# Row projections of a two-mixer block: two of 512 columns in place of four of 256

## The chip, the cores and the metric

The kernel runs on one core of one Trainium2 chip. The metric is the device time of one launch in microseconds (us). The kernel before the change has a median of 2136.6 us over 3 runs (2136.44 to 2136.79).

## The reference

The program computes a block of two layers and then a second block of another kind, for 512 tokens of width 1024, in fp32. The change touches only the mixers of the two layers of the first block:

```
h = rms_norm(x, attn_norm_w[layer])
proj = h @ w_in[layer]              # 1024 -> 12 groups of 256 columns
a_q, a_i, a_zf, a_zb, a_g, b_u, c_q, c_k, c_v = split(proj)   # 256 each, the three c_* 512
o_a = hgrn2_mixer(a_q, a_i, a_zf, a_zb, a_g, lb)   # gated recurrence, both directions, chunks of 64
o_b = fourier_mixer(b_u)                           # real part of a 2-D DFT
o_c = dilated_attention_mixer(c_q, c_k, c_v)       # rotary on q and k, softmax attention
x = x + concat(o_a, o_b, o_c) @ w_out[layer]
x = x + square(relu(rms_norm(x) @ w_up[layer])) @ w_down[layer]
```

Most results of the projection are wanted with channels on the partitions. Three are wanted with tokens on the partitions ("rows"): `a_i` (the values of the recurrence), `b_u` (input of the DFT) and `c_v` (the values of the attention), 1024 columns in all.

## The kernel before, in words

**Projections.** fp32 products are made of three fp32r products. ScalarE copies each weight tile to a rounded part (`WH`, function `act_hi`), VectorE subtracts it from the raw weight for the rest (`WL`, `dve_lo`), and TensorE adds high*high, low*high and high*low. A weight *chunk* is 128 x 2048 (1 MB); SyncE loads it into one of two `raw` slots. A chunk is two *units* of 1024 columns, and there are three places for finished units (`NUNIT = 3`): unit u can be made once TensorE has let go of unit u-3. ScalarE and VectorE make a unit 1.06 and 1.2 us at a time, and TensorE waits for it by the semaphore `w_lo`. A projection (`lin`) of 256 columns takes one chunk.

`pe_lin` works in four *projection steps* of 12 matmuls of 512 columns: unit 0 into result tile 0, unit 0 into tile 1, then unit 1 into each. `pe_rows`, where the tokens are the stationary operand and the weights move, also has four steps, of 24 matmuls of 256 columns. In both a unit is let go after two steps, so a new unit is wanted every second step.

**One mixer.** Its projections are, in order: `head` = two gates, two silu, and the rows of `a_i`; `tail` = two for q, two for k (kind `copy`), the rows of `b_u`, and two rows projections for `c_v`. That is 12 projections, 24 units (numbered 0 to 23 here) and 48 projection steps (0 to 47). Units 8 and 9 are those of `a_i`, 10 to 17 those of q and k, 18 and 19 those of `b_u`, 20 to 23 those of `c_v`. ScalarE evicts rows from PSUM with a factor per token (`act_made`).

Beside them runs the recurrence, as sixteen *level steps*: levels -1 to 6, in two halves each (`rec_pe`, `rec_act`, `rec_dve`, `rec_pool`). In a level step TensorE makes scores (16 matmuls of 128 columns), VectorE merges them (`copy_predicated`, line 154) and makes the operands of the next level from exponentials of ScalarE. At level 6 ScalarE, not VectorE, evicts the scores. Then follow four transposes-and-sum steps: the turned keys ("kt", which ScalarE evicts), the chunk states ("st", which needs `a_i`), the outputs ("o"), the sums and the inverse roots. After the last projection step come the DFT (`four_pe`) and the attention.

**What sets the order.** Each engine has an order of its own, written out by hand as a string: a `u` is one step of the projections and what goes with them, a `c` one step of the recurrence. TensorE follows `MIX_PE`, VectorE `MIX_DVE`, ScalarE and GpSimd `MIX`. On ScalarE and VectorE every second `u` has work: evict the finished projection (if there is one) and make one unit, two ahead. So in the last two groups of the eight, ScalarE's order is: level 5 first half (the two exponentials for level 6), level 5 second half, evict q/k, unit 18; level 6 first half (evict its scores), unit 19; level 6 second half, evict, unit 20. VectorE's is: level 4 second half, low part of unit 17; level 5 first half, low part of 18; level 5 second half; level 6 first half, low part of 19. TensorE's is: steps 32, 33; level 5 first half; 34; level 5 second half; 35, 36; level 6 first half; 37; level 6 second half; 38, 39, 40; kt; 41; st; 42, 43, 44; o; 45; sum; 46, 47; DFT.

**The rotary exchange.** q and k are multiplied in place, and their halves of 32 partitions are exchanged by DMAs of SyncE (`sp_turn`, line 1458), which stand in SyncE's queue between the chunk loads: after the load of chunk n comes the exchange of projection n-3. The rotation works of VectorE and GpSimd stand at fixed units (`ROT = 14`).

**Banks.** A projection has two of the four PSUM banks 0 to 3, by the parity of its number (`BANK`). `clear` waits until the bank's last holder is evicted, and `four_pe` waits for the last rows projections in the same way before it writes banks 0 to 3.

Of the kernel before, what the change touches and what calls it, by code (L numbers as in the profile page):

```python
# [12 lines left out]
ACT = mybir.ActivationFunctionType  # L13
# [210 lines left out]
def build(nc, I, out):  # L224
    ctx = ExitStack()
    with ctx:
# [82 lines left out]
        def lin(src, kind, to=None, j=0, ly=0):  # L309
            lins.append(Lin(len(lins), [chunk(x) for x in src], kind, to, j, ly))  # L310
            return lins[-1]
# [13 lines left out]
        def mix_memory(ly):  # L325
# [37 lines left out]
            m.ms, m.rs, m.ris = (small[:, 256 + 32 * i:288 + 32 * i] for i in range(3))  # L363
            W = I["w_in"][ly]
            m.head = [lin([W[2, 0]], "gate", j=0, ly=ly), lin([W[3, 0]], "gate", j=1, ly=ly),
                      lin([W[0, 0]], "silu", m.aq2, ly=ly), lin([W[4, 0]], "silu", m.ag2, ly=ly),
                      lin([W[1, 0]], "rows", m.ai3, ly=ly)]
            m.tail = [lin([W[6 + j, 0]], "copy", m.cq3[:, 2 * j:2 * j + 2], ly=ly) for j in range(2)]
            m.tail += [lin([W[8 + j, 0]], "copy", m.ck3[:, 2 * j:2 * j + 2], ly=ly) for j in range(2)]
            m.tail += [lin([W[5, 0]], "rows", m.u3, ly=ly)]  # L370
            m.tail += [lin([W[10 + j, 0]], "rows", m.cv3[:, :, 256 * j:256 * j + 256], ly=ly) for j in range(2)]
            m.dft = chunk(I["dft"], "raw")
            m.out = [lin([I["w_out"][ly][j, 0]], "res", (m.scratch, 2 * ly), j, ly) for j in range(4)]
            f = m.ffn = Mix()
# [127 lines left out]

        BANK, BEFORE, holder = {}, {}, {}
        for l in lins:
            for m in range(2):
                b = (2 * (l.n - s2.low[0].n) + m) % 3 if l.kind in ("lat", "shift", "keep") else l.n % 2 * 2 + m
                BANK[l.n, m], BEFORE[l.n, m] = b, holder.get(b)
                holder[b] = (l, m)

# [34 lines left out]
        def pe_lin(e, l):  # L544
            for ci, n in enumerate(l.chunks):
                u0 = chunks[n][2]
                for h in range(2):
# [4 lines left out]
                    for m in range(2):  # L552
# [15 lines left out]
                            t.then_inc(*did("w_use", u))  # L568
                        yield

        def pe_rows(e, l):

            u0 = chunks[l.chunks[0]][2]
            for h in range(2):
                e.wait_ge(*at("w_lo", u0 + h))
                wh, wl = unit(u0 + h)
                for m in range(2):
                    if h == 0:
                        clear(e, l, m)
                    for tk in (2 * m, 2 * m + 1):  # L580
                        o = bank_of(l, m)[:, tk % 2 * 256:(tk % 2 + 1) * 256]
                        for k in range(4):
                            xh, xl, made = operand(l, h * 4 + k)
                            e.wait_ge(*at(*made))
                            xh, xl = xh[:, tk * 128:(tk + 1) * 128], xl[:, tk * 128:(tk + 1) * 128]
                            ws = slice(k * 256, (k + 1) * 256)
                            e.mm(o, xh, wh[:, ws], h + k + tk % 2 == 0, False)
                            e.mm(o, xl, wh[:, ws], False, False)
                            t = e.mm(o, xh, wl[:, ws], False, h + k + tk % 2 == 5)
                    if h:  # L590
                        t.then_inc(*did("lin_mm", l.n, m))
                    elif m:
                        t.then_inc(*did("w_use", u0))
                    yield

        def pe_lins(e, ls):
            for l in ls:
                yield from pe_rows(e, l) if l.kind == "rows" else pe_lin(e, l)

        def act_made(e, l):  # L600

            for m in range(2):
                ps = bank_of(l, m)
                if l.kind in ("gate", "silu"):
                    sg = mixes[l.ly].sg[m]
                    e.wait_ge(*at("lin_dve", "ps", l.n, m))
                    if l.kind == "silu":
                        p = lins[l.n - 1]
                        e.wait_ge(*at("lin_dve", "sg" if p.kind == "gate" else "out", p.n, m))
                    e.act(sg, sg if l.kind == "gate" else l.to[:, m, :], ACT.Sigmoid).then_inc(*did("lin_act", "sg", l.n, m))  # L610
                elif l.kind == "rows":
                    e.wait_ge(*at("lin_mm", l.n, m))
                    e.wait_ge(*at("nrm_dve", 2 * l.ly - 1, "col"))
                    for i in range(2):
                        t = e.act(l.to[:, 2 * m + i, :], ps[:, i * 256:(i + 1) * 256], ACT.Copy,
                                  rcol[:, 2 * m + i:2 * m + i + 1])
                    t.then_inc(*did("lin_act", "ps", l.n, m))
                elif l.kind == "copy":
                    e.wait_ge(*at("lin_mm", l.n, m))
                    e.act(l.to[:, m, :], ps, ACT.Copy).then_inc(*did("lin_act", "ps", l.n, m))  # L620
                elif l.kind == "keep":
                    e.wait_ge(*at("lin_dve", "ps", l.n, m))
                    e.act(s2.keep[m], s2.keep[m], ACT.Sigmoid).then_inc(*did("lin_act", "keep", l.n, m))
                elif l.kind == "hid":
                    f, half = l.to
                    t = 2 * l.j + m
                    e.wait_ge(*at("ffn_dve", l.ly, half, "sq", t))
                    e.act(f.hh[:, t, :], f.rl[m], ACT.Copy).then_inc(*did("ffn_act", l.ly, half, "hi", t))
                elif l.kind == "res" and l.to[1] is not None:
                    act_next(e, l, m)  # L630
# [121 lines left out]
        def side_lins(e, ls, made, split, late):  # L752
# [3 lines left out]
            for l in ls:  # L756
                for n in l.chunks:
                    for h in range(2):
                        if late:
                            yield  # L760
                        if before is not None:
                            made(e, before)
                            before = None
                        u = chunks[n][2] + h + 2
                        if u < len(units) and units[u][0] <= n + 1:
                            split(e, u)
# [145 lines left out]
        def rec_pe(e, x):  # L912
# [32 lines left out]
                        t = e.tr(b[:, ch * 128:(ch + 1) * 128], x.kl[dr][:, (hp * 4 + ch) * 128:(hp * 4 + ch + 1) * 128], ident)  # L945
                    t.then_inc(*did("rec_pe", ly, "kt", dr, hp))
            yield
            e.wait_ge(*at("lin_act", "ps", x.head[4].n, 1))
            for dr in range(2):
                for hp in range(2):  # L950
                    e.wait_ge(*at("rec_act", ly, "kt", dr, hp))
# [268 lines left out]
        def four_pe(e, x, first_scores):  # L1220
# [4 lines left out]
            for part in range(2):  # L1225
                w = slot(n)[:, part * 768:(part + 1) * 768]
                for d in range(2):
                    b, ds = bk(part * 2 + d), slice(d * 128, (d + 1) * 128)
                    l = x.tail[-1 if part else -2]
                    e.wait_ge(*emptied(l, 1))  # L1230
                    e.wait_ge(*emptied(x.tail[-1], 1))
                    e.mm(b[:, 0:128], x.u04[:, ds], w[:, 0:128])
                    e.mm(b[:, 256:384], x.u24[:, ds], w[:, 128:256])
                    for k in range(2):
# [273 lines left out]
        def win_pool(e, x):  # L1508
            yield from between(range(48), **{f"s{ROT + i}": lambda i=i: rot_pool(e, x, i) for i in range(8)})

        MIX = "u" * 12 + "c" + "uu" + "cucuu" * 8 + "cuu" * 4 + "cuuuc"
        MIX_DVE = "u" * 12 + "c" + "uu" + "cuucu" * 8 + "cuu" * 4 + "cuuuc"
        MIX_PE = "u" * 16 + "c" + "cucuu" * 8 + "cu" * 2 + "cuuu" + "cu" + "cuuuc"

# [1517 lines left out]
        def sp_program(e):  # L3032
# [5 lines left out]
            for n in range(2, len(chunks)):  # L3038
# [15 lines left out]
                if 0 <= fixed < 4:  # L3054
                    for i in range(2 * fixed, 2 * fixed + 2 + fixed // 3):
                        sp_expert(e, i)
                if n - 3 in lin_of_chunk and lin_of_chunk[n - 3] in turned_lins:
                    sp_turn(e, lin_of_chunk[n - 3])
                if n < s2.wr2_c[0] and n - 3 in lin_of_chunk and lin_of_chunk[n - 3].kind == "keep":
                    sp_keep(e, lin_of_chunk[n - 3])  # L3060
            for k in range(4):
# [255 lines left out]
def layout(inp):  # L3317
# [6 lines left out]
    a["w_out"] = np.stack([lay(g["w_out"][i], 8, 256) for i in range(2)])  # L3324
    a["w_up"] = np.stack([lay(g["w_up"][i], 8, 256) for i in range(2)])
    a["w_down"] = np.stack([lay(g["w_down"][i], 8, 256) for i in range(2)])
    q = {k[:-2]: x[0] for k, x in g.items() if k.endswith("_2")}
    a["pos2"] = np.ascontiguousarray(g["positions_2"][0])
    w = q["w_in"]
# [42 lines left out]
```

## Time and profile before

| what | us |
|---|---|
| median of three runs | 2136.6 |
| the profiled execution's own time | 2136.76 |
| its span, first to last instruction | 2135.0 |
| TensorE busy | 2072.6 (97%) |
| VectorE busy | 1183.8 (55%) |
| ScalarE busy | 734.7 (34%) |
| GpSimd busy | 133.1 (6%) |
| mean granted TensorE clock | 0.991 of full speed |
| layer 0: steps of the recurrence beside the projections | 59.79 to 185.11 |

Times inside the profile are counted from the start of the span. In a row of the timeline the first number is the start, the second the length, xN the number of instructions merged in it, and [x <-engine tile line] says that the engine sat idle for x us before it and what ended that. A row's count depends on where the asked stretch ends, its start doesn't. Matmuls overlap (each is shown some 0.39 us long and the next starts 0.23 us later), so a distance is read from start to start.

### The profile page before, as it was taken

To read this page: it belongs to the slowest core of one execution; us is meant where nothing else is said; L and a number is where in the kernel's file an instruction comes from. 1 tells how busy PE (TensorE), PEld (TensorE's weight loads), DVE (VectorE), ACT (ScalarE), POOL (GpSimd) and SP (SyncE) were. 2 spreads that over 40 slices of the span, in tenths; PEclk is the share of its full clock that TensorE was granted. 3 is DMA by queue.
4 is the path that set the end of the run, shared out by engine and by line. 5 is a ranking of instruction groups with operands and counts; after the bars stand their busy time and mean duration, and the time that the engine had idled before them with its cause. 6 is when DMAs were issued, how large, how long until landed. Compare 5 with 4: busy or idle time off the path is not lost.

```text
span 2135.0 us, 32294 instructions
## 1 busy us (share of the span) xinstructions
PE 2072.6 (97%) x13784; PEld 1561.1 (73%) x13784; DVE 1183.8 (55%) x1878; ACT 734.7 (34%) x1139; POOL 133.1 (6%) x112
## 2 busy tenths in 40 slices
PE   8999999999999999999999999999999999999997
PEld 6886688888888886688888887566688856944543
DVE  8886555435535886555325445475743345444545
ACT  6445642212233445633212333234422123311112
POOL 1220010000010220010000020000000000100000
PEclk9999999999999999999999999999999999999998
DMA  5222022222222222022222222211211036299993
GB/s 194 70 83 76 11 95 99 99 99 99 99 91 86 70 85 80 21 81 97 99 99 99 99 99 79 85 56 56 78 61 62 32 129 261 106 419 419 379 420 155
DMA packets 47139, 263.08 MB, mean 123 GB/s; under 512 B 7064, under 2 KB 7320, under 8 KB 18960
## 3 DMA queue, kind: packets, MB, share of 16 engines
q1 hardware_dynamic: 44400, 256.46, 32.3%
q0 software_dynamic: 2160, 4.17, 0.5%
q8 instruction: 111, 1.82, 0.4%
q10 hardware_dynamic: 432, 0.34, 0.1%
q14 instruction: 36, 0.29, 0.0%
HBM read 251.01 MB, written 9.44 MB: 122 GB/s over the span
## 4 chain that ended last, share of the span: by engine, by line
PE 86%; DVE 8%; ACT 3%; issue 1%; DMA 1%; SPq 0%; DVEq 0%; ACTq 0%; POOLq 0%
PE psum L121 83%; DVE A_mix L134 3%; PE psum L124 2%; ACT A_mix L128 1%; DVE WL L134 1%; DVE A_second L134 1%; ACT A_mix L131 1%; DVE A_second L142 1%; DVE A_mix L160 1%; ACT WH L128 1%; DVE A_mix L154 1%; DMA A_mix<-A_mix 0%; DMA experts<-h_rows,A_second 0%; SPq L166 0%; DVE HL L134 0%
## 5 line engine op out<-in xcount | busy, mean ns | idle before, releaser
L134 DVE TENSOR_TENSOR WL<-raw,WH 128x1024 fp32r<-128x1024 f32 x236 | 300.9, 1277 | 351.5 <-ACT WH L128 351.0
L128 ACT ACTIVATE WH<-raw 128x1024 fp32r<-128x1024 f32 x236 | 247.5, 1054 | 355.5 <-PE psum L121 340.0
L121 PE MATMUL psum<-HH,WH 128*128 128x512 f32 x736 | 299.7, 407 | 17.7 <-DVE HL L142 10.2
L121 PE MATMUL psum<-R_op,WH 128*128 128x512 f32 x1024 | 315.9, 390 | 0.0
L121 PE MATMUL psum<-R_ffn,WH 128*128 128x512 f32 x1024 | 315.1, 389 | 0.0
L121 PE MATMUL psum<-HL,WH 128*128 128x512 f32 x736 | 288.5, 392 | 0.0
L121 PE MATMUL psum<-HH,WL 128*128 128x512 f32 x736 | 288.4, 392 | 0.0
L121 PEld LDWEIGHTS psum<-R_op,WH 128*128 128x128 f32 x1024 | 192.2, 188 | 40.7 <-issue 1.0
L121 PEld LDWEIGHTS psum<-R_ffn,WH 128*128 128x128 f32 x1024 | 192.2, 188 | 40.0
L121 PE MATMUL psum<-R_ffn,WL 128*128 128x512 f32 x512 | 199.2, 389 | 0.0
L121 PE MATMUL psum<-R_op,WL 128*128 128x512 f32 x512 | 199.2, 389 | 0.0
L121 PEld LDWEIGHTS psum<-HH,WH 128*128 128x128 f32 x736 | 138.9, 189 | 63.9 <-DVE WL L134 16.6
L121 PEld LDWEIGHTS psum<-HH,WL 128*128 128x128 f32 x736 | 139.0, 189 | 30.0
L121 PEld LDWEIGHTS psum<-HL,WH 128*128 128x128 f32 x736 | 139.3, 189 | 28.6 <-issue 1.9
L121 PE MATMUL psum<-A_second 64*64 64x64 f32 (+4 forms) x3736 | 154.1, 233 | 5.5 <-DVE A_second L154 2.5
L121 PEld LDWEIGHTS psum<-A_second 64*64 64x64 f32 (+3 forms) x3736 | 124.3, 137 | 35.4 <-issue 23.7
L121 PE MATMUL psum<-A_mix 128*64 128x128 f32 (+4 forms) x1408 | 126.0, 315 | 7.8 <-DVE small L160 3.7
L128 ACT ACTIVATE A_second<-psum 128x512 f32<-128x512 f32 (+3 forms) x109 | 52.4, 502 | 194.0 <-PE psum L121 177.8
L134 DVE TENSOR_TENSOR A_mix<-A_mix 128x512 f32<-128x512 f32 (+2 forms) x150 | 112.5, 800 | 10.2 <-DMA A_mix<-A_mix 8.7
L121 PEld LDWEIGHTS psum<-R_op,WL 128*128 128x128 f32 x512 | 96.1, 188 | 20.0
L121 PEld LDWEIGHTS psum<-R_ffn,WL 128*128 128x128 f32 x512 | 96.1, 188 | 19.9
L121 PEld LDWEIGHTS psum<-A_mix 128*64 128x64 f32 (+2 forms) x1408 | 80.3, 161 | 37.3 <-issue 19.2
(217 smaller groups left out, 2662.3 us busy)
## 6 DMA issues: line engine op xcount, KB each, us to landing
raw<-in_w_in SPq DMA_DIRECT2D x41, 1024.0 KB, 4.9
raw<-in_w_up SPq DMA_DIRECT2D x32, 1024.0 KB, 4.9
raw<-in_w_down SPq DMA_DIRECT2D x32, 1024.0 KB, 4.9
A_second<-in_w_gu SPq DMA_DIRECT2D x31, 1024.0 KB, 15.0
A_second<-in_w_dn SPq DMA_DIRECT2D x23, 1024.0 KB, 18.8
experts<-in_w_gu SPq DMA_DIRECT2D x23, 1024.0 KB, 15.5
raw<-in_w_out SPq DMA_DIRECT2D x12, 1024.0 KB, 4.9
X<-in_w_gu SPq DMA_DIRECT2D x10, 1024.0 KB, 17.0
```

The lines of the kernel that those rows point to most:

```text
L121: return self.raw.matmul(o, l, r, start=start, stop=stop)
L124: return self.raw.matmul(o, i, ident, is_transpose=True, start=True, stop=True)
L128: return self.raw.activation(o, i, f, scale=scale)
L131: return self.raw.activation(o, i, f, scale=scale, bias=bias, accum_out=accum)
L134: return self.raw.tensor_tensor(o, a, b, op)
L142: return self.raw.scalar_tensor_tensor(o, a, s, b, op0, op1)
L154: return self.raw.copy_predicated(o, m, a)
L160: return self.raw.tensor_tensor_reduce(o, a, b, scale, 3.0e38, ADD, MIN, accum)
```

## The change

The four rows projections of a layer become two of 512 columns each, behind q and k: the first gives `a_i` and `b_u` together, the second all of `c_v`. Their weights come from a new array `w_row` (the same bytes in another layout, in chunks of 4 times 128 rows by 512 columns, two chunks per projection). Projections per layer are 10, chunks, units and projection steps stay 12, 24 and 48: q and k now take units 8 to 15, the rows units 16 to 23 (steps 32 to 47).

`pe_rows` now has eight steps for its four units, each step one unit into two token tiles, 12 matmuls of 512 columns, in the order `ROW_PIECES` (unit, first tile): a rows projection uses all four banks. The pairs of tiles finish in the order (2, 3), (0, 1). ScalarE evicts tiles 2 and 3 at the projection's last unit (`act_rows`) and 0 and 1 with the next projection's first.

`MIX` (ScalarE and GpSimd) has its seventh group changed from `cucuu` to `uuccu`: two `u` are moved ahead of level 5. `MIX_DVE` and `MIX_PE` are as they were. The exchange stands after the load of chunk n for projection n-4. The recurrence's states and the DFT wait for the new projections.

```
-                      lin([W[0, 0]], "silu", m.aq2, ly=ly), lin([W[4, 0]], "silu", m.ag2, ly=ly),
-                      lin([W[1, 0]], "rows", m.ai3, ly=ly)]
+                      lin([W[0, 0]], "silu", m.aq2, ly=ly), lin([W[4, 0]], "silu", m.ag2, ly=ly)]
             m.tail = [lin([W[6 + j, 0]], "copy", m.cq3[:, 2 * j:2 * j + 2], ly=ly) for j in range(2)]
             m.tail += [lin([W[8 + j, 0]], "copy", m.ck3[:, 2 * j:2 * j + 2], ly=ly) for j in range(2)]
-            m.tail += [lin([W[5, 0]], "rows", m.u3, ly=ly)]
-            m.tail += [lin([W[10 + j, 0]], "rows", m.cv3[:, :, 256 * j:256 * j + 256], ly=ly) for j in range(2)]
+            for j, to in enumerate(((m.ai3, m.u3), (m.cv3,))):
+                m.tail.append(lin([I["w_row"][ly, j, k] for k in range(2)], "rows", to, ly=ly))
...
+        ROWS = (2, 3, 0, 1)
+        ROW_PIECES = ((0, 0), (1, 0), (0, 2), (1, 2), (2, 2), (3, 2), (2, 0), (3, 0))
         def pe_rows(e, l):
+            us = [chunks[n][2] + h for n in l.chunks for h in range(2)]
+            for i, tk0 in ROW_PIECES:
+                e.wait_ge(*at("w_lo", us[i]))
+                wh, wl = unit(us[i])
+                for tk in (tk0, tk0 + 1):
+                    if i == 0:
+                        clear(e, l, tk)
+                    o, ts = bank_of(l, tk), slice(tk * 128, (tk + 1) * 128)
+                    for k in range(2):
+                        xh, xl, made = operand(l, 2 * i + k)
+                        ws = slice(k * 512, (k + 1) * 512)
+                        e.mm(o, xh[:, ts], wh[:, ws], i + k == 0, False)
+                        e.mm(o, xl[:, ts], wh[:, ws], False, False)
+                        t = e.mm(o, xh[:, ts], wl[:, ws], False, i == 3 and k == 1)
+                    if i == 3:
+                        t.then_inc(*did("lin_mm", l.n, tk))
+                    elif tk == (3, 3, 1)[i]:
+                        t.then_inc(*did("w_use", us[i]))
+                yield
...
+        def act_rows(e, l, tks):
+            e.wait_ge(*at("nrm_dve", 2 * l.ly - 1, "col"))
+            for tk in tks:
+                ps, w = bank_of(l, tk), S // len(l.to)
+                e.wait_ge(*at("lin_mm", l.n, tk))
+                for i, to in enumerate(l.to):
+                    t = e.act(to[:, tk, :], ps[:, i * w:(i + 1) * w], ACT.Copy, rcol[:, tk:tk + 1])
+                t.then_inc(*did("lin_act", "ps", l.n, tk))
...
+                        if made is act_made and l.kind == "rows" and (n, h) == (l.chunks[-1], 1):
+                            act_rows(e, l, ROWS[:2])
...
-            e.wait_ge(*at("lin_act", "ps", x.head[4].n, 1))
+            e.wait_ge(*at("lin_act", "ps", x.tail[4].n, 1))
...
-                    l = x.tail[-1 if part else -2]
-                    e.wait_ge(*emptied(l, 1))
-                    e.wait_ge(*emptied(x.tail[-1], 1))
+                    e.wait_ge(*emptied(x.tail[-1], 1 if part else 3))
...
-        MIX = "u" * 12 + "c" + "uu" + "cucuu" * 8 + "cuu" * 4 + "cuuuc"
+        MIX = "u" * 12 + "c" + "uu" + "cucuu" * 6 + "uu" + "ccu" + "cucuu" + "cuu" * 4 + "cuuuc"
...
-                if n - 3 in lin_of_chunk and lin_of_chunk[n - 3] in turned_lins:
-                    sp_turn(e, lin_of_chunk[n - 3])
+                if n - 4 in lin_of_chunk and lin_of_chunk[n - 4] in turned_lins:
+                    sp_turn(e, lin_of_chunk[n - 4])
```

## Rows read from the trace of the kernel before

**Rows 1.** The page: span, TensorE's busy time, and the chain that ended last

```profile
span 2135.0 us, 32294 instructions
...
PE 2072.6 (97%) x13784; PEld 1561.1 (73%) x13784; DVE 1183.8 (55%) x1878; ACT 734.7 (34%) x1139; POOL 133.1 (6%) x112
...
PE 86%; DVE 8%; ACT 3%; issue 1%; DMA 1%; SPq 0%; DVEq 0%; ACTq 0%; POOLq 0%
```

**Rows 2.** Groups by form: the matmuls of 256 columns, one of three alike

```profile
L121 PE MATMUL psum<-WH,HH 128*128 128x256 f32 x256 | 74.2, 290 | 0.0
```

**Rows 3.** Timeline of TensorE, layer 0, levels and projections

```profile
63.94 0.83 PE L121 MATMUL psum<-A_mix 64*128 64x128 f32 x10
...
70.98 1.16 PE L121 MATMUL psum<-A_mix 64*128 64x128 f32 x16
...
77.64 0.50 PE L121 MATMUL psum<-HH,WH 128*128 128x512 f32 x1 [1.35 <-DVE WL L134]
...
98.15 1.16 PE L121 MATMUL psum<-A_mix 64*128 64x128 f32 x16
...
104.91 1.16 PE L121 MATMUL psum<-A_mix 64*128 64x128 f32 x16
...
126.51 0.71 PE L121 MATMUL psum<-A_mix 64*128 64x128 f32 x8
...
130.55 1.16 PE L121 MATMUL psum<-A_mix 64*128 64x128 f32 x16
...
137.88 1.16 PE L121 MATMUL psum<-A_mix 64*128 64x128 f32 x16 [0.35 <-DVE A_mix L134]
...
142.04 1.16 PE L121 MATMUL psum<-A_mix 64*128 64x128 f32 x16
...
151.87 1.94 PE L124 MATMUL psum<-C,A_mix 128*128 128x128 f32 x16
...
156.60 1.62 PE L121 MATMUL psum<-A_mix 128*64 128x64 f32 x48
...
167.27 0.80 PE L121 MATMUL psum<-A_mix 128*64 128x128 f32 x8 [0.22 <-DVE A_mix L142]
...
185.11 2.86 PE L121 MATMUL psum<-raw,A_mix 128*128 128x128 f32 x16 [1.02 <-ACT A_mix L128]
```

**Rows 4.** The same view in layer 1: the DFT's first matmuls

```profile
823.85 1.33 PE L121 MATMUL psum<-raw,A_mix 128*128 128x128 f32 x7 [1.02 <-ACT A_mix L128]
```

**Rows 5.** Timeline of VectorE, layer 0: low parts of units 17 and 19

```profile
124.34 1.21 DVE L134 TENSOR_TENSOR WL<-raw,WH 128x1024 fp32r<-128x1024 f32 x1
...
141.72 1.22 DVE L134 TENSOR_TENSOR WL<-raw,WH 128x1024 fp32r<-128x1024 f32 x1 [2.66 <-ACT WH L128]
```

**Rows 6.** Timeline of ScalarE, layer 0: evictions and high parts

```profile
139.04 1.56 ACT L128 ACTIVATE A_mix<-psum 64x256 f32<-64x256 f32 x4 [6.87 <-PE psum L121]
140.63 1.06 ACT L128 ACTIVATE WH<-raw 128x1024 fp32r<-128x1024 f32 x1
...
154.43 1.60 ACT L128 ACTIVATE A_mix<-psum,small 128x256 f32<-128x256 f32 x4
158.93 2.01 ACT L128 ACTIVATE WH<-raw 128x1024 fp32r<-128x1024 f32 x2 [2.90 <-DMA raw<-in_w_in]
```

**Rows 7.** Timeline of TensorE, two long waits elsewhere in the program

```profile
1518.36 0.50 PE L121 MATMUL psum<-HH,WH 128*128 128x512 f32 x1 [2.86 <-DVE A_second L134]
...
2094.19 6.59 PE L121 MATMUL psum<-experts 128*64 128x512 f32 x16 [3.27 <-issue]
```

**Rows 8.** Windows: busy PE, PEld, DVE, ACT, POOL (count), then clock, DMA, GB/s

```profile
1380.00:1385.00 5.00, 3.08 (x10) 1.52 (x9) 3.71 (x5) 0.00 (x0) 0.00 (x0) 1.00 0.37 125
1385.00:1390.00 5.00, 5.00 (x18) 3.11 (x17) 4.93 (x8) 1.06 (x1) 0.00 (x0) 1.00 0.81 298
...
1520.00:1525.00 5.00, 5.00 (x17) 3.91 (x16) 3.92 (x5) 4.16 (x6) 0.00 (x0) 0.67 0.24 93
...
2095.00:2100.00 5.00, 5.00 (x14) 1.58 (x12) 0.00 (x0) 0.00 (x0) 0.00 (x0) 0.50 0.11 44
```

More of the change, by code:

```diff
@@ L504, in build @@
         for l in lins:
-            for m in range(2):
-                b = (2 * (l.n - s2.low[0].n) + m) % 3 if l.kind in ("lat", "shift", "keep") else l.n % 2 * 2 + m
+            for m in range(4 if l.kind == "rows" else 2):
+                b = (2 * (l.n - s2.low[0].n) + m) % 3 if l.kind in ("lat", "shift", "keep") else (l.n % 2 * 2 + m) % 4
                 BANK[l.n, m], BEFORE[l.n, m] = b, holder.get(b)
@@ L569, in pe_lin @@
                         yield
+        ROWS = (2, 3, 0, 1)
+        ROW_PIECES = ((0, 0), (1, 0), (0, 2), (1, 2), (2, 2), (3, 2), (2, 0), (3, 0))
         def pe_rows(e, l):
[L573 to L594, printed above, removed]
@@ new lines, in pe_rows @@
+            us = [chunks[n][2] + h for n in l.chunks for h in range(2)]
[8 more added lines that the diff above has]
+                        xh, xl, made = operand(l, 2 * i + k)
+                        e.wait_ge(*at(*made))
+                        ws = slice(k * 512, (k + 1) * 512)
[7 more added lines that the diff above has]
+                yield
@@ L598, in pe_lins @@
                 yield from pe_rows(e, l) if l.kind == "rows" else pe_lin(e, l)
+        def act_rows(e, l, tks):
[6 more added lines that the diff above has]
+                t.then_inc(*did("lin_act", "ps", l.n, tk))
         def act_made(e, l):
+            if l.kind == "rows":
+                act_rows(e, l, ROWS[2:])
+                return
             for m in range(2):
@@ L610, in act_made @@
                     e.act(sg, sg if l.kind == "gate" else l.to[:, m, :], ACT.Sigmoid).then_inc(*did("lin_act", "sg", l.n, m))
[L611 to L617, printed above, removed]
                 elif l.kind == "copy":
@@ L3326, in layout @@
     a["w_down"] = np.stack([lay(g["w_down"][i], 8, 256) for i in range(2)])
+    a["w_row"] = np.stack([lay(np.concatenate([w[:, 256:512], w[:, 1280:1536], w[:, 2560:3072]], 1), 4, 512)
+                           for w in (g["w_in"][i] for i in range(2))])
     q = {k[:-2]: x[0] for k, x in g.items() if k.endswith("_2")}
```

## The prediction

> **What bounds the kernel now.** Start with the page [rows 1]: TensorE is busy for 97% of the span and the chain that ended last lies on it for 86%, so a change pays by what it takes from TensorE's time, and costs by what it makes TensorE wait. That is an average over stages, so the second view is TensorE's timeline of one mixer [rows 3]. From 63.94 to 185.11 us the engine has four waits, all small: 1.35 us at 77.64 for a unit's low part, 0.35 at 137.88 for an operand of level 6, 0.22 at 167.27 for a chunk state and 1.02 at 185.11 for an eviction ahead of the DFT. Layer 1 repeats it 638.7 us later [rows 4], so one layer is worked out and doubled. The third view is how near VectorE and ScalarE are. The low part of unit 19 ends at 142.94 (141.72 + 1.22) [rows 5], and TensorE's step 38, its first user, begins some 1.1 us behind the level step at 142.04 [rows 3]: 0.2 us to spare. That near miss decides this case. Unit preparation is just in time, so a schedule that wants a unit one step sooner waits.
>
> **The matmuls.** 768 matmuls of 256 columns (three forms of 256, one shown [rows 2]) become 384 of 512, with the same columns streamed. Their cost can't be read from the mean of 290 ns, since neighbours overlap; it is read between starts. From the level step at 63.94 to the one at 70.98 are one level step and two projection steps of 48 matmuls of 256: 7.04 us. From 98.15 to 104.91 are the same with 24 of 512: 6.76 us [rows 3]. So a replaced pair saves 0.28 / 24 = 11.7 ns, 192 pairs of a layer 2.2 us, both layers 4.5 us. One step of 512 is 6.76 - 4.04 = 2.72 us (4.04 is 126.51 to 130.55, a level step and one step), which leaves 1.32 for a level step with its switch.
>
> The Trainium skill ("TensorE: Matmul & The Clock Gate", the section on 56 ns against 53.3 ns) puts the fixed part of a start-to-start distance at about 2.5 ns for a warm matmul. By that, the 384 removed matmuls are worth 1.0 us, an estimate, and the time below would be 3.5 us higher. The trace shows 11.7 ns, and for this pattern the trace is taken.
>
> **Where the new steps want their units.** Before, every unit had two steps, so unit 17 was wanted at step 34, unit 19 at step 38. With `ROW_PIECES` the units of a rows projection are wanted at its steps 0, 1, 4 and 5: unit 16 at step 32, 17 at 33, 18 at 36, 19 at 37, then 20 at 40, 21 at 41, 22 at 44, 23 at 45. Each second unit comes a step early. TensorE's and VectorE's lists are unchanged, so I walk layer 0 through the level steps.
>
> *To 119.75.* `a_i`'s four steps become q's, worth 0.5 us (0.28 for two, 0.11 for each single one). But the wait at 77.64 hangs on evictions and a unit on ScalarE and VectorE, which only partly move with TensorE. I let 0.35 us through (bounds 0 and 0.5), and VectorE's later work, which waits on level steps several times, moves with it.
>
> *Unit 17.* Its low part ended at 125.55 (124.34 + 1.21) [rows 5]; in VectorE's unchanged list it stands behind the merges of level 4's second half. Less 0.35 it is there at 125.2. Step 33 would have begun at 126.51 - 0.35 - 2.72 = 123.4. TensorE waits 1.8 us, and a step after a wait takes 4.04 - 1.1 = 2.95, so level 5 begins at 125.25 + 2.95 = 128.2 instead of 126.51. Bounds: 1.2 (if VectorE's rotation ahead of it shrinks) to 2.2.
>
> *Level 6.* Two level steps and three steps later (4.04 and 6.76) its first half begins at 139.0 instead of 137.88: the wait of 0.35 there is gone and step 36 is shorter. The two `u` that `MIX` moves ahead of level 5 bring unit 18 forward. ScalarE made it behind two exponentials, now before, so it is no longer late for step 36.
>
> *Unit 19.* This is the costly one. On ScalarE the unit's high part stands behind the eviction of level 6's first half, in the old list and in the new one: the changed group ends a `u` before it. Its chain is fixed: TensorE's scores begin at 137.88, the eviction runs from 139.04 to 140.60, the high part from 140.63 to 141.69 [rows 6], the low part from 141.72 to 142.94 [rows 5]. That is 5.06 us from the scores' start. Before, step 37 and the other half of the level filled this time. Now step 37 itself wants unit 19, and in TensorE's strict order level 6's second half, whose inputs are there, stands behind it. Step 37 would begin 1.1 us after the scores' start, so TensorE idles 4.0 us. The second half begins at 139.0 + 5.1 + 2.95 = 147.05 instead of 142.04. Bounds: 3.7 to 4.3.
>
> *Then* the distances go on with the shorter steps: to "kt" 1.32 + 3 x 2.72 = 9.48, so 156.5 (before 151.87); to "st" 4.73 - 0.11 = 4.62, so 161.15 (156.60); to "o" 10.67 - 0.35 - 0.22 = 10.1, so 171.25 (167.27); to the DFT 17.84 less 0.4 for three steps and less the wait of 1.02, so 187.7 (185.11) [rows 3]. That last wait goes because part 0 of the DFT now asks only for tiles 2 and 3, evicted two steps before the end. Net 2.6 us per layer later: about 3.4 won, 6.0 lost.
>
> **What could be late next, costed at nothing.** "st" now needs `a_i`, evicted behind kt: in the old trace four evictions of this kind end at 156.03 (154.43 + 1.60), 4.2 us after kt began [rows 6], and TensorE comes to "st" 4.6 us after it; a slip costs up to 1 us. Units 20 and 21 hang on the second half of level 6 and move with it; by the same durations they are ready about 1.4 us before steps 40 and 41. Unit 22's chunk lands late already (ScalarE waited 2.90 us for it at 158.93 [rows 6]), and with the exchange's rotations pushed some 3 us it is ready near 164.3 against step 44 at 168. SyncE's queue keeps its order: the exchange moves one projection and one chunk, so it stands behind the same load as before, and asks for results that are there sooner. GpSimd's rotation of tile 2 now comes before level 6's product and adds about 1.5 us to it; the product is wanted at 139 and is there near 135.
>
> **The clock.** TensorE has two long waits elsewhere [rows 7]: 2.86 us, after which the window 1520 to 1525 has a granted clock of 0.67, and 3.27 us, after which 2095 to 2100 has 0.50, the lower level of 1.2 GHz throughout [rows 8]. The wait of 1.9 us between 1380 and 1385 (3.08 of 5 us busy) left it at 1.00 [rows 8]. A wait of 4.0 us in a dense stage is longer than both that were followed by a fall, so I charge one fall for unit 19: 5 x (1 - 0.67) = 1.65 us, bounds 0 and 2.5 (5 x 0.50). For unit 17's 1.8 us I charge none. The Trainium skill (the same page, its section on HAM oscillation) warns of just this: TensorE starts again at half rate after an idle gap between bursts. The two rows agree.
>
> Sum per layer 2.6 + 1.6 = 4.2 us, both 8.3 us with rounding. Against the profiled execution's own 2136.76 (span 2135.0) that is 2145.1; that execution is 0.16 above the median, so 2145.0.
>
> **Rivals.**
> *Waits without a fall of the clock:* +5.1, 2141.7. For it: the falls may depend on where a wait lies. Against: both long waits of the trace had one.
> *The first wait lowers the clock too, or the later units slip by as much:* 3.2 more, 2148.1. Against: the wait of 1.9 us that cost nothing.
> *Only unit 19's wait:* unit 17 is in time and TensorE is held 0.5 us by level 6's operand instead; no fall. 2.6 - 2.0 + 0.5 = 1.1 per layer, 2138.7.
> *Faster, no wait at the early units:* the shorter matmuls and the freed eviction come through. It holds if ScalarE makes unit 19 ahead of level 6's eviction, at least 4 us sooner than its list as I read it allows. Then a layer gains 2.6 - 2.0 + 0.5 - 3.9 = -2.8, the time is 2130.9. For it: a third place lets unit 19 be made as soon as unit 16 is let go, after step 34, and its chunk is there. Against: engines here take their work in order, and eviction and high part stand 0.03 us apart in that order [rows 6].
>
> **How the numbers follow.** Forecast 0.48, waits without a fall 0.16, more falls or slips 0.14, only unit 19's wait 0.10, faster 0.12. A measurement of this kernel tells 0.2% (4.3 us) from no change. Slower: 0.48 + 0.14 and 0.13 of the second case, 0.75. Same: the rest of it and most of the fourth, 0.12. Faster 0.13. The range 2138.5 to 2149.5 leaves out the faster case, nearly half of the fourth and a tail above; the likeliest case alone is 2143 to 2147.5.
>
> **What would show it.** In TensorE's timeline after: a wait of about 1.8 us, ended by `WL`, near 125 and one of about 4.0 us near 140 to 144, the same two 640 us later, followed by a window of clock 0.6 to 0.8 near 145 to 150; no wait before the DFT; forms of 256 columns gone and 128 more of each of three forms of 512; ScalarE's high part of unit 19 right behind four evictions. If the span is about 6 us shorter and these waits are missing, the reading of ScalarE's order is wrong. If they are there and the time is under 2141, the clock's share is.

## The result, and the profile after

The changed kernel is slower: median 2142.03 us over 7 runs (2141.28 to 2147.55), the kernel before 2135.28 over 7 (2130.13 to 2136.79). The ratio is 1.0041, with a 95% interval of 1.0031 to 1.0052, so 6.6 to 11.1 us. It is worked out from all executions and not from the two medians, which are 6.8 us apart; the means, 2143.2 and 2134.4, are 8.8 apart. A second group of runs gave 1.0052 (1.0039 to 1.0065). The forecast was 8.3 us more than before and 2145.0; the profiled execution took 2146.67.

The page first: fewer matmuls, TensorE as busy as before, a longer span. Busy TensorE says nothing of what was lost.

```profile
span 2144.9 us, 31518 instructions
...
PE 2074.8 (97%) x13400; PEld 1545.2 (72%) x13400; DVE 1185.1 (55%) x1878; ACT 733.8 (34%) x1131; POOL 134.4 (6%) x112
```

TensorE's timeline of layer 0 answers to [rows 3]. The columns are start, length, what ran, and in brackets the idle time before it with what ended it:

```profile
59.11 1.16 PE L121 MATMUL psum<-A_mix 64*128 64x128 f32 x16
...
63.15 1.05 PE L121 MATMUL psum<-A_mix 64*128 64x128 f32 x14
...
69.91 1.16 PE L121 MATMUL psum<-A_mix 64*128 64x128 f32 x16
...
77.22 0.51 PE L121 MATMUL psum<-HH,WH 128*128 128x512 f32 x1 [2.10 <-DVE WL L134]
...
84.48 1.16 PE L121 MATMUL psum<-A_mix 64*128 64x128 f32 x16
...
126.80 0.50 PE L121 MATMUL psum<-WH,HH 128*128 128x512 f32 x1 [1.76 <-DVE WL L134]
...
129.74 1.16 PE L121 MATMUL psum<-A_mix 64*128 64x128 f32 x16
...
140.54 1.16 PE L121 MATMUL psum<-A_mix 64*128 64x128 f32 x16
...
145.68 0.50 PE L121 MATMUL psum<-WH,HH 128*128 128x512 f32 x1 [3.98 <-DVE WL L134]
...
150.22 1.16 PE L121 MATMUL psum<-A_mix 64*128 64x128 f32 x16
...
190.63 0.60 PE L121 MATMUL psum<-raw,A_mix 128*128 128x128 f32 x4
```

The two waits stand where they were forecast: 1.76 us for unit 17 (1.8 forecast), 3.98 us for unit 19 (4.0). The level steps at 63.15 and 69.91 are 6.76 us apart (7.04 before), and no wait stands before the DFT. Layer 1 has the same two:

```profile
769.39 0.50 PE L121 MATMUL psum<-WH,HH 128*128 128x512 f32 x1 [1.78 <-DVE WL L134]
...
789.83 0.79 PE L121 MATMUL psum<-WH,HH 128*128 128x512 f32 x1 [3.98 <-DVE WL L134]
```

Unit 19's chain, ScalarE's timeline and VectorE's row behind it, answers to [rows 5, 6]. The eviction begins when TensorE has made the scores, the high part 0.02 us behind it, the low part behind that; 145.63 is the end, and 145.68 TensorE's start:

```profile
141.73 1.56 ACT L128 ACTIVATE A_mix<-psum 64x256 f32<-64x256 f32 x4 [10.28 <-PE psum L121]
143.31 1.06 ACT L128 ACTIVATE WH<-raw 128x1024 fp32r<-128x1024 f32 x1
...
144.40 1.23 DVE L134 TENSOR_TENSOR WL<-raw,WH 128x1024 fp32r<-128x1024 f32 x1 [2.94 <-ACT WH L128]
```

ScalarE had idled for 10.28 us before it. That its list alone held it back is what `early19` below shows.

The windows answer to [rows 8] (busy PE, PEld, DVE, ACT, POOL, then the granted clock, DMA share, GB/s). The clock falls behind the waits of 3.98 us in both layers, and in this execution behind the wait of 2.10 us near 77 and that of 1.78 us near 769 too. Behind unit 17's 1.76 us in layer 0 it stays at 1.00:

```profile
75.00:80.00 5.00, 2.90 (x11) 2.26 (x9) 4.83 (x8) 3.14 (x3) 0.00 (x0) 0.80 0.00 2
80.00:85.00 5.00, 5.00 (x25) 3.85 (x26) 3.13 (x5) 2.89 (x4) 1.83 (x2) 0.86 0.62 210
...
125.00:130.00 5.00, 3.24 (x17) 2.44 (x18) 5.00 (x9) 0.82 (x1) 0.00 (x0) 1.00 0.09 22
...
145.00:150.00 5.00, 4.32 (x12) 3.31 (x12) 4.97 (x6) 1.38 (x3) 0.00 (x0) 0.66 0.18 41
...
770.00:775.00 5.00, 5.00 (x28) 3.67 (x26) 2.95 (x5) 2.11 (x2) 0.45 (x1) 0.66 0.22 52
...
790.00:795.00 5.00, 5.00 (x12) 3.63 (x12) 4.47 (x5) 0.53 (x2) 0.00 (x0) 0.52 0.22 52
```

At the DFT layer 0 is 5.5 us late (190.63 against 185.11). The forecast without clock is 2.6 of it, and two falls of 1.6 us are the rest but for 0.3. The falls can be read from the distances: from the end of the wait near 77 to the next level step it is 7.26 us (77.22 to 84.48) against 5.67 before, and from the end of unit 19's wait to level 6's second half 4.54 us (145.68 to 150.22), against 2.94 behind unit 17's wait, where the clock stayed up. Two rows of the kernel before belong to this, its first level step and the one behind the wait:

```profile
59.79 1.16 PE L121 MATMUL psum<-A_mix 64*128 64x128 f32 x16
...
83.31 1.16 PE L121 MATMUL psum<-A_mix 64*128 64x128 f32 x16
```

Counted from the first level step (59.11 and 59.79), the layer takes 6.2 us longer: the 0.7 us by which TensorE came sooner to this stage went into the longer wait near 77.

### The profile page after: what moved, and what is told of

The parts are those of the page before. It is cut to its first block, busy times and chain, and to the rows that moved or that the text cites. A ratio compares the mean times of both kernels' runs of the same rounds, so it can differ in the third digit from the quotient of the medians.

```text
span 2144.9 us, 31518 instructions
## 1 busy us (share of the span) xinstructions
PE 2074.8 (97%) x13400; PEld 1545.2 (72%) x13400; DVE 1185.1 (55%) x1878; ACT 733.8 (34%) x1131; POOL 134.4 (6%) x112
## 3 DMA queue, kind: packets, MB, share of 16 engines
q8 instruction: 108, 1.77, 0.3%
## 4 chain that ended last, share of the span: by engine, by line
PE 86%; DVE 7%; ACT 4%; DMA 1%; issue 1%; SPq 0%; DVEq 0%; ACTq 0%; POOLq 0%
PE psum L121 84%; PE psum L124 2%; DVE A_mix L134 1%; DVE WL L134 1%; ACT A_mix L128 1%; DVE A_second L134 1%; ACT A_mix L131 1%; ACT WH L128 1%; DVE A_second L142 1%; DMA M<-in_m 1%; DVE A_mix L160 0%; DMA experts<-h_rows,A_second 0%; DVE A_mix L154 0%; ACT branch_gates L131 0%; DVE HL L134 0%
```

## The experiments

Each is compared with the kernel before on the same chip; ratios are those of the times, worked out from all executions. "Faster than the changed kernel" goes by the difference of two such ratios. A stretch of a trace is one execution. The theory is that of the prediction: units wanted a step early, and places in the lists. The rivals are named with each run.

**The changed kernel again** (`same`), no edit.

> The changed kernel again, as the anchor of this group. Both theories: 5 to 8 us slower than before, with TensorE waits of 1.8 and 4.0 us in layer 0 for the low parts of units 17 and 19, and the same in layer 1.

2144.56 us, 1.0052. The waits in its trace are 1.77 and 3.98 us. This is the anchor for the three runs that follow (`two_steps`, `fill`, `mix_old`).

**Two steps for each unit** (`two_steps`).

```
-ROW_PIECES = ((0, 0), (1, 0), (0, 2), (1, 2), (2, 2), (3, 2), (2, 0), (3, 0))
+ROW_PIECES = ((0, 0), (0, 2), (1, 0), (1, 2), (2, 2), (2, 0), (3, 2), (3, 0))
```

> ROW_PIECES with two steps in a row for each unit, as in the kernel before; all else of the change stays. Theory (units wanted a step early): the waits for units 17 and 19 are gone, 5.8 us per layer less waiting. But tiles 2 and 3 of the first rows projection then finish one step later (step 38), ScalarE evicts them only behind level 6's exponentials, near 150.8, and step 40 wants their banks near 148.5: a new wait of 1.5 to 3 us per layer, ended by ScalarE. In all 6 to 8 us faster than the changed kernel, 0 to 2 us faster than before. Rival (the loss comes from the wider rows projections themselves, their four banks and their late a_i, not from the order of the units): still 4 us or more slower than before.

2132.23 us, 0.9996 (0.9986 to 1.0005): some 12 us faster than the changed kernel, level with before. The 6 to 8 us expected counted the waits alone; in this trace the clock does not fall in layer 0 either. TensorE's timeline in layer 0 has no wait for units 17 and 19; what is late next is the PSUM banks, and by 0.27 us GpSimd:

```profile
137.55 0.71 PE L121 MATMUL psum<-A_mix 64*128 64x128 f32 x8 [0.27 <-POOL A_mix L134]
...
149.49 0.47 PE L121 MATMUL psum<-WH,HH 128*128 128x512 f32 x1 [1.03 <-ACT A_mix L128]
...
155.79 0.50 PE L121 MATMUL psum<-WH,HH 128*128 128x512 f32 x1 [1.54 <-ACT A_mix L128]
```

Step 40 waits 1.03 us for tiles 2 and 3, where 1.5 to 3 were forecast; step 41 waits another 1.54 for tiles 0 and 1, which I had not seen. So the order of the units carries the loss; the wider rows projections and the late `a_i` do not. It also shows what the change's order buys: it frees the banks sooner, and pays for that in units.

**Matmuls of no use in the waits** (`fill`): in `pe_rows` for the first rows projection, and 6 likewise ahead of unit 10.

```
+                if len(l.to) == 2:
+                    for _ in range({(1, 0): 7, (3, 2): 16}.get((i, tk0), 0)):
+                        e.mm(bk(7), HHt[:, 0, 0:128], HHt[:, 0, :])
                 e.wait_ge(*at("w_lo", us[i]))
```

> The changed kernel with matmuls of no use (512 columns, into bank 7, which nobody reads then) where TensorE waits: 6 before unit 10 (1.4 us), 7 before unit 17 (1.6 us), 16 before unit 19 (3.6 us), in each layer. Theory (waits cost their length, and a fall of the clock on top): the units arrive at the same times, so the waits' length stays in the time; the granted clock stays at 1.00 from 60 to 190 us, and each fall that the changed kernel has there is worth about 1.6 us: 2 to 6 us faster than the changed kernel on average, and no executions at 2147. Rival (the clock is of no account): same time as the changed kernel within 1 us, or slower by the filling.

2138.1 us, 1.0023: about 6 us faster than `same` (1.0052) with 58 matmuls more, and no execution above 2139.6. Its windows, against those above:

```profile
75.00:80.00 5.00, 5.00 (x33) 3.77 (x32) 4.67 (x7) 3.83 (x5) 0.00 (x0) 1.00 0.02 5
80.00:85.00 5.00, 5.00 (x34) 3.95 (x33) 4.04 (x7) 2.21 (x3) 1.15 (x1) 1.00 0.53 169
...
145.00:150.00 5.00, 5.00 (x33) 3.94 (x34) 4.48 (x5) 1.53 (x5) 0.00 (x1) 1.00 0.22 52
```

The granted clock stays at 1.00, which is 2.4 GHz. Level 6's second half now begins 8.09 us behind its first half (139.68 to 147.77), against 9.68 in the changed kernel. From the first level step to the DFT, both layers together, `fill` takes 255.44 us where the kernel before takes 250.66: 4.8 us more, and the forecast without a fall was 5.1. So the loss has two parts, both shown: the waits' length, which `fill` keeps, and the falls of the clock, which it takes away.

**The old order of ScalarE and GpSimd** (`mix_old`).

```
-MIX = "u" * 12 + "c" + "uu" + "cucuu" * 6 + "uu" + "ccu" + "cucuu" + "cuu" * 4 + "cuuuc"
+MIX = "u" * 12 + "c" + "uu" + "cucuu" * 8 + "cuu" * 4 + "cuuuc"
```

> The changed kernel with the old order of ScalarE and GpSimd (the group cucuu eight times). Theory: unit 18 is made behind level 6's exponentials again, ready near 134 to 135, and step 36, held back by the wait for unit 17, wants it near 136: within 1 us of the changed kernel, the waits for units 17 and 19 unchanged. Rival (the moved steps are what makes ScalarE late for unit 19): the wait for unit 19 shrinks by 1 us or more and the kernel is 2 us or more faster than the changed one.

2144.15 us, 1.0055: no difference that can be measured. The waits of 1.76 and 3.98 us stay, so the moved steps are not what makes unit 19 late. But a third one appears, which I had not forecast:

```profile
130.83 0.50 PE L121 MATMUL psum<-WH,HH 128*128 128x512 f32 x1 [1.08 <-ACT A_mix L128]
```

That is step 34, which wants the banks of the last k projection. The moved steps bring that eviction ahead of the exponentials; unit 18 merely comes with it. In the traces this is worth 1.1 us in layer 0: from the level step ahead of unit 17's wait to level 6's first half it is 20.76 us here (119.77 to 140.53) and 19.62 in the changed kernel (120.92 to 140.54). The times do not resolve that much.

**Unit 19 ahead of level 6** (`early19`): ScalarE on a list of its own with `"uccuu"` for its last group, VectorE with `"ucucu"` for its eighth.

> The changed kernel with unit 19 made ahead of level 6's first half in ScalarE's and VectorE's lists (GpSimd's stays); ROW_PIECES as changed. Theory (ScalarE's place for unit 19 behind the eviction of level 6 makes the 4.0 us): that wait falls to 1.5 us or less, the wait of 1.8 us for unit 17 stays, and a new wait of some 1 us for ScalarE's eviction shows at step 40. In all 4 to 8 us faster than the changed kernel, near before (within 3 us). Rival (the wait is set by the weights' load or the place in memory, not by the list): the wait stays at 4 us and the time is the changed kernel's.

2133.19 us, 0.9997 (0.9987 to 1.0007): some 9 to 12 us faster than the changed kernel (1.0041, 1.0052), above the 4 to 8 expected. Level 6's halves start at 139.70 and 143.74, the 4.04 us of a level step and a step without a wait. Unit 17 still costs 1.78 us, and step 40 waits 1.70 us for the eviction (0.17 in layer 1):

```profile
125.92 0.50 PE L121 MATMUL psum<-WH,HH 128*128 128x512 f32 x1 [1.78 <-DVE WL L134]
...
139.70 1.16 PE L121 MATMUL psum<-A_mix 64*128 64x128 f32 x16
...
143.74 0.49 PE L121 MATMUL psum<-A_mix 64*128 64x128 f32 x4
...
152.27 0.47 PE L121 MATMUL psum<-WH,HH 128*128 128x512 f32 x1 [1.70 <-ACT A_mix L128]
```

The list was the cause of unit 19's wait; neither the load nor the place in memory held it.

**Halved matmuls** (`half_width`): in `pe_rows` each of the three matmuls is made twice, on 256 columns.

> The changed kernel with each matmul of 512 columns in the rows projections made as two of 256; steps, units and order stay. Theory (11.7 ns for each matmul saved, and nearly all of these steps on the path): distances of the rows steps grow by 0.14 us each, 3.5 to 4.5 us slower than the changed kernel. Rival (a fixed 2.5 ns per matmul): 1 us slower. The waits for units 17 and 19 stay (1.7 and 4.0 us).

2142.18 us, 1.0043 (1.0028 to 1.0059): the time does not tell it from the changed kernel (1.0041, 1.0052), and so decides nothing between the theories; the 3.5 to 4.5 us expected did not show. The distances between level steps do: 4.16 and 7.04 us (128.28, 132.44, 139.48), against 4.04 and 6.76 with whole matmuls. These are before's distances, so the width alone makes them.

```profile
128.28 1.16 PE L121 MATMUL psum<-A_mix 64*128 64x128 f32 x16
...
132.44 1.16 PE L121 MATMUL psum<-A_mix 64*128 64x128 f32 x16
...
139.48 1.16 PE L121 MATMUL psum<-A_mix 64*128 64x128 f32 x16
```

**The DFT's old wait** (`dft_wait`): both parts wait for `emptied(x.tail[-1], 1)`.

> The changed kernel with the old wait of the DFT: both parts wait for the last tiles of the last rows projection. Theory (the freed wait is worth its length): a wait of 0.7 to 1.1 us, ended by ScalarE, stands before the DFT's first matmul in each layer. Rival (ScalarE is done by then anyway, since its last eviction is one of 512 columns in place of two of 256): a wait under 0.3 us. One look, so only the trace is to be read.

In the one execution a wait of 0.87 us, ended by ScalarE, is back. It was 1.02 with two evictions of 256 columns [rows 3]. The freed wait is real, and a little smaller than I counted it.

```profile
191.84 0.35 PE L121 MATMUL psum<-raw,A_mix 128*128 128x128 f32 x1 [0.87 <-ACT A_mix L128]
```

**Four edits together** (`best1`): the two lists of `early19`; for the first rows projection, the one with two results (`len(l.to) == 2`), two steps in a row for each of its first two units, so that unit 17 is wanted at step 34, and the order of the changed kernel for the rest; and there the eviction of tiles 2 and 3 behind unit 20, at the first half of the last chunk.

```
+        FIRST_PIECES = ((0, 0), (0, 2), (1, 0), (1, 2), (2, 2), (3, 2), (2, 0), (3, 0))
...
+            for i, tk0 in FIRST_PIECES if len(l.to) == 2 else ROW_PIECES:
...
-                        if made is act_made and l.kind == "rows" and (n, h) == (l.chunks[-1], 1):
+                        if made is act_made and l.kind == "rows" and len(l.to) == 1 and (n, h) == (l.chunks[-1], 1):
...
                             split(e, u)
+                        if made is act_made and l.kind == "rows" and len(l.to) == 2 and (n, h) == (l.chunks[-1], 0):
+                            act_rows(e, l, ROWS[:2])
```

> early19 with two more edits: the first rows projection takes its first two units two steps each, so unit 17 is wanted at step 34; ScalarE evicts its tiles 2 and 3 right behind unit 20 and ahead of level 6's last exponentials. Theory: no wait for unit 17, at most 1 us for unit 19, none or under 0.5 us at step 40. 3 to 6 us faster than before in all, the gain of the shorter matmuls and of the freed wait. Rival (something else of the change costs as much, the later a_i or the four banks): within 2 us of before.

2130.55 us, 0.9986 (0.9973 to 0.9999), 0.2 to 5.8 us faster than before. The forecast waits are gone, but level 6 waits 1.85 us for GpSimd:

```profile
140.39 0.83 PE L121 MATMUL psum<-A_mix 64*128 64x128 f32 x10 [1.85 <-POOL A_mix L134]
```

The rotation that `MIX` moves ahead waits for its exchange until 131.95, and level 6's product (two operations) stands behind it. GpSimd's timeline, the rotation and then the product:

```profile
131.95 3.16 POOL L134 TENSOR_TENSOR A_mix<-A_mix 128x512 f32<-128x512 f32 x1 [9.32 <-DMA A_mix<-A_mix]
...
135.05 5.28 POOL L134 TENSOR_TENSOR A_mix<-A_mix 128x512 f32<-128x512 f32 x2
```

The product ends at 140.33, and TensorE starts at 140.39. In the changed kernel the same three operations start at the same time:

```profile
131.95 1.30 POOL L134 TENSOR_TENSOR A_mix<-A_mix 128x512 f32<-128x512 f32 x1 [9.32 <-DMA A_mix<-A_mix]
...
133.20 3.96 POOL L134 TENSOR_TENSOR A_mix<-A_mix 128x512 f32<-128x512 f32 x2
```

There they end at 137.16, 3.4 us before level 6's first half begins at 140.54, and would have been in time in `best1` too, where TensorE was there at 138.54. So the place in the list alone does not make this wait: the operations themselves take longer, 3.16 and 5.28 us against 1.30 and 3.96. VectorE works beside them. Its low part of unit 18 took 2.14 us in the changed kernel, where it began behind GpSimd's rotation, and 1.21 us in `best1`, where it began ahead of it:

```profile
132.19 2.14 DVE L134 TENSOR_TENSOR WL<-raw,WH 128x1024 fp32r<-128x1024 f32 x1
```

```profile
131.53 1.21 DVE L134 TENSOR_TENSOR WL<-raw,WH 128x1024 fp32r<-128x1024 f32 x1
```

`two_steps` has the same picture: the low part began at 130.23 and took 1.22 us, the rotation began at 130.67 and took 3.15, and level 6 waited 0.27 us for GpSimd. That the overlap makes the operations longer is read from these rows; no run tests it by itself.

**GpSimd on the old order** (`best_pool`): `best1` with `MIX` as in `mix_old`; ScalarE keeps its own list.

> best1 with GpSimd on the old order (rotation of tile 2 behind level 6's product again). best1's trace had a new wait of 1.85 us for GpSimd at level 6's first half. Theory (the moved steps of MIX make GpSimd late, hidden in the changed kernel by the wait for unit 17): that wait falls to 0.4 us or less in both layers, 2 to 4 us faster than best1, 5 to 8 us faster than before. Rival (unit 19 or VectorE's operand is late next, at the same place): a wait of the same size for VectorE stands there and the time is best1's.

2128.28 us, 0.9968 (0.9957 to 0.9980). Level 6's wait is 0.22 us, for VectorE. GpSimd starts at 128.91, with the product first and the rotation behind it, at 132.40:

```profile
128.91 5.23 POOL L134 TENSOR_TENSOR A_mix<-A_mix 128x512 f32<-128x512 f32 x3 [7.76 <-ACT A_mix L128]
```

Two waits of VectorE's low parts are left:

```profile
77.31 0.50 PE L121 MATMUL psum<-HH,WH 128*128 128x512 f32 x1 [1.47 <-DVE WL L134]
...
149.16 0.50 PE L121 MATMUL psum<-WH,HH 128*128 128x512 f32 x1 [1.01 <-DVE WL L134]
```

**Unit 10 ahead of the second silu** (`best3`: in `side_lins` the unit is made before the eviction where a silu projection was the last).

> best_pool with unit 10 made ahead of the second silu's eviction on ScalarE and VectorE. Theory (unit 10 is late only by its place behind that eviction, and TensorE's 1.5 to 2.1 us there now and then lower the clock): the wait at unit 10 goes, 3 to 6 us faster than best_pool and 8 to 12 us faster than before. Rival (the recurrence's chain on VectorE is late anyway): a wait of 1 us or more moves to the next level step (level 1), and the time is within 1.5 us of best_pool.

2125.3 us, 0.9955 (0.9943 to 0.9967): 7 to 12 us faster than before, the fastest version here. The wait at 77 is halved, and is now for an operand of VectorE:

```profile
76.31 0.47 PE L121 MATMUL psum<-HH,WH 128*128 128x512 f32 x1 [0.71 <-DVE A_mix L134]
...
148.19 0.50 PE L121 MATMUL psum<-WH,HH 128*128 128x512 f32 x1 [1.08 <-DVE WL L134]
```

The gain over `best_pool` is 2.8 us (0.9968 to 0.9955), below the 3 forecast and with overlapping intervals.

**The same in the kernel before** (`before_silu`).

> The kernel before with unit 10's move alone. Theory: the same edit gives the kernel before 2.5 to 5 us (the wait of 1.35 us in both layers, and the falls of the clock behind it where there are any). Rival (level 1 is late instead): under 1 us.

2128.66 us, 0.9972 (0.9962 to 0.9982), 6 us faster than before: more than forecast. From 60 to 84 us TensorE has no wait at all. So a part of what `best3` has over before is owed to an edit that has nothing to do with the rows projections. How large it is depends on the order in which the two are counted, since their gains do not add up:

| | by the ratios, us | first level step to DFT, both layers, us |
|---|---|---|
| before | | 250.66 |
| unit 10's move alone (`before_silu`) | 6.0 faster | 247.96 |
| repaired change alone (`best_pool`) | 6.8 faster | 245.99 |
| both (`best3`) | 9.6 faster | 243.81 |

By the ratios the repaired change adds 3.6 us on top of unit 10's move, with intervals that overlap by a little, and the move adds 2.8 on top of the repaired change. In the traces the move is worth 2.2 to 2.7 us and the repaired change 4.2 to 4.7. The 6 us of `before_silu` hold more than that. Its executions have a mean clock of 0.993, those of the kernel before 0.991, and by the 1.4 us for each 0.001 given below that is some 3 us more, an estimate; whether the move brings this by sparing falls of the clock is not shown.

**Halved matmuls where nothing hides them** (`best3_half`).

> best3 with the rows projections' matmuls halved to 256 columns, as in half_width, where the waits for units 17 and 19 are out of the way. Theory (11.7 ns for each of 384 matmuls): 3.5 to 4.5 us slower than best3, so 5 to 6 us faster than before. Rival (a fixed 2.5 ns each): 1 us slower than best3. Distances of the rows steps 0.12 to 0.16 us longer each by the theory, 0.03 by the rival.

2127.48 us, 0.9973 (0.9963 to 0.9983). By the ratios that is 3.8 us slower than `best3`, but in another group of runs and with 2 us of interval on each. The traces say less: single steps are 0.12 us longer each, but from the level step ahead of the rows projections to the DFT of layer 0 it is only 0.74 us more (118.43 to 182.75, against 118.41 to 181.99), because the wait of 1.08 us for unit 20 is gone in the halved kernel. The first steps of the DFT, in `best3` and in the halved one:

```profile
181.99 1.47 PE L121 MATMUL psum<-raw,A_mix 128*128 128x128 f32 x8
```

```profile
182.75 0.83 PE L121 MATMUL psum<-raw,A_mix 128*128 128x128 f32 x5
```

So the widths give 1.8 us a layer to TensorE, and VectorE takes some 1.1 back. The net number lies between 1.5 us (twice 0.74) and 3.8 for both layers, and the times alone do not tell it from the rival's 1 us; it is the distances that are too long for a fixed 2.5 ns per matmul.

## Why the prediction held, point by point

*Bound and method.* Walking one mixer's level steps gave the place of both waits, and their length to within 0.1 us: they are 1.8 and 4.0 us by the forecast, and 1.76 and 3.98 in layer 0 of the changed kernel, 1.77 and 3.98 in `same`, 1.76 and 3.98 in `mix_old`. `two_steps` shows that both come from the order of the units, `early19` that the second hangs on the place in ScalarE's and VectorE's lists.

*Matmuls.* 11.7 ns a pair is what the distances show, before and after. Behind the two waits of the changed kernel the shorter steps come through: from "st" to the DFT it is 26.21 us (164.42 to 190.63) against 28.51 (156.60 to 185.11), 2.3 less, with 1.24 of it from the waits of 0.22 and 1.02 that are gone. What the width is worth by itself was counted too high for the repaired kernel: where VectorE paces TensorE again, as at unit 20 in `best3`, over half is given back (0.74 of 1.82 us is left).

*The DFT's wait.* Freed as forecast, 0.87 us and not 1.02.

*To 119.75.* I let 0.35 us through; TensorE left the wait at 77 0.42 us sooner. But the wait itself grew from 1.35 to 2.10 us in the profiled execution (1.46 in `half_width`, 1.74 in `same`), and behind 2.10 the clock fell. I had charged no fall there. The sooner TensorE reaches this stage, the longer it waits: the first level step stands at 59.11 us with the wait of 2.10, at 59.44 with 1.74 (`same`) and at 60.16 with 1.47 (`mix_old`), while ScalarE's exponentials ahead of unit 10 start between 70.19 and 70.23 in all three. So this wait takes up what TensorE gains ahead of it.

*What could be late next.* "st", units 20 to 22 and SyncE's queue cost nothing in the changed kernel, as forecast; but the chunk of unit 22 landed 5.4 us later than before (its high part began at 164.33, before at 158.93), where some 3 were forecast. GpSimd's product was put near 135; in the changed kernel it was ready at 137.16, still 3.4 us ahead of level 6. In `best1` it was ready at 140.33 and cost 1.85 us; that its operations take so much longer when VectorE comes first was in no term. And I read the moved `u` of `MIX` as bringing unit 18; what step 34 needs of it is the eviction.

*The clock.* One fall per layer was charged. The profiled execution had two per layer; that others had fewer is inferred from their clocks: at a mean clock of 0.990 to 0.992 the changed kernel took 2141.3 to 2142.1, at 0.987 2146.7 and 2147.6. The forecast was added to 2136.6, and over seven executions the kernel before has a median of 2135.28. Added to that, the forecast gives 2143.6 and the rival without a fall 2140.4; the median of 2142.03 lies half-way. By the ratio the difference is 8.7 us, close to the forecast's 8.3. So the waits, their places and their lengths were right by the mechanism; that the clock's share of 3.3 us came out near is in part luck, since the number of falls changes from execution to execution and falls elsewhere move both kernels. `fill` puts the share at some 6 us in its group of runs.

## What to carry to other kernels

When a loop is regrouped, list for each prepared tile the step that first wants it, before and after. Here equal counts hid that each second unit was wanted one step sooner, in a schedule with 0.2 us to spare. A transfer or a tile is as early as its place in the list of the engine that makes it, and an engine that idled for 10 us ahead of it is the sign of a wrong place. Freeing one wait shows the next (units, then banks, then GpSimd), so repair them in one walk, and read how long each operation takes again once its neighbours have moved. Test an unrelated edit alone and on top of the change: here the gains of the two did not add up.

## What the runs showed of the hardware

Executions of one kernel differ mostly with the clock. Over 81 executions of the kernel before, beside the experiments in four groups, the time ran from 2127.5 to 2140.2 us and fell by 1.4 us for each 0.001 of mean granted clock (correlation -0.83). A fall is no fixed price of a wait. Near 77 a wait of 1.47 us (`best_pool`) and one of 1.74 us (`same`) left the clock at 2.4 GHz, and the one of 2.10 us in the changed kernel was followed by a fall. But behind unit 17's wait of 1.78 us the clock stayed up in layer 0 of `early19` and fell in layer 1 of the changed kernel, and 1.77 us in layer 0 of `same` was followed by a fall (0.66 from 125 to 130) where 1.76 us in the changed kernel was not. So the length alone does not decide it. The two falls in layer 0 of the changed kernel cost 1.6 us each. Keeping TensorE busy with matmuls of no use across the waits was worth 6 us, though every one was pure extra work.

The Trainium skill ("TensorE: Matmul & The Clock Gate", the section on HAM oscillation) says that a long enough wait between two bursts of matmuls makes TensorE start the next one at its lower clock. The windows from 145 to 150 us agree with it: 0.66 in the changed kernel, 1.00 in `fill`, which leaves no such gap there.

Where VectorE and GpSimd work at the same time, one of them can take longer. The same GpSimd rotation took 1.30 us in the changed kernel and 3.16 in `best1`, and the same VectorE subtraction 2.14 and 1.21; in both cases the longer one had started later. When one of the two lists moves, the durations on the other engine have to be read again.
